# A banded-attention pass: v and the first scores moved ahead of the products with v, those put inside the k projection, half of the next x asked for later

## The reference, cut to what matters

```python
h = rms_norm(x, ln_g[l])
proj = jnp.einsum('bsd,de->bse', h, w_in[l])
(u_pool, g_pool, c_a, c_b, g_conv, q, k, v, g_attn) = split_columns(proj)
...
y_attn = sliding_window_attention(q, k, v, attn_sinks[l])   # 8 heads, 2 kv heads, window 128, ALiBi, sinks
y = jnp.concatenate([y_pool * jax.nn.silu(g_pool), y_conv * jax.nn.silu(g_conv), y_attn * jax.nn.silu(g_attn)], axis=-1)
x = x + jnp.einsum('bse,ed->bsd', y, w_out[l])
return rms_norm(x, final_g)
```

## Time and profile before

| | |
|---|---|
| median of 3 runs | 1409.57 us (1408.69 to 1409.6) |
| the profiled execution | 1410.81 us |
| its span, first to last instruction | 1409.1 us |
| mean granted TensorE clock | 0.991 of full speed |
| PE busy | 1362.0 us of the span |
| DVE busy | 1143.6 us of the span |

### The profile page before, as it was taken

The page is one execution under the profiler, slowest core; times in us unless marked ns, Lnnn a source line. Parts: engine busy times, 40 slices in busy tenths (PEclk is TensorE's granted clock), DMA queues, the critical chain, the costliest instruction groups (busy, mean ns, idle before and its releaser), DMA issues.

```text
span 1409.1 us, 20603 instructions
## 1 busy us (share of the span) xinstructions
PE 1362.0 (97%) x7070; PEld 1115.8 (79%) x7070; DVE 1143.6 (81%) x2173; ACT 550.5 (39%) x1421; POOL 480.5 (34%) x745
## 2 busy tenths in 40 slices
PE   6999999999999999989999999999999999999998
PEld 5778777777778787768888888888888888888886
DVE  5787868686868685629899998988999998898886
ACT  5665656564646463412112122121232333333332
POOL 5363636272726362530101011010110355455552
PEclk9999999999999999999999999999999999999999
DMA  9749494949494848774203133031327575554531
GB/s 214 217 124 316 125 325 112 314 129 309 126 295 146 252 153 199 284 158 180 115 35 135 37 129 134 15 134 59 144 97 261 232 249 169 180 179 158 169 106 75
DMA packets 117547, 239.18 MB, mean 170 GB/s; under 512 B 17488, under 2 KB 75216, under 8 KB 109776
## 3 DMA queue, kind: packets, MB, share of 16 engines
q1 hardware_dynamic: 93312, 214.24, 45.8%
q10 hardware_dynamic: 24144, 23.80, 7.0%
HBM read 139.44 MB, written 98.57 MB: 169 GB/s over the span
## 4 chain that ended last, share of the span: by engine, by line
PE 70%; DVE 13%; DMA 10%; SPq 3%; issue 2%; POOL 1%; ACT 0%; POOLq 0%; DVEq 0%; ACTq 0%
PE wide L346 12%; PE wide L348 12%; PE wide L347 12%; DMA p_scratch<-a_rows 7%; PE pair L1290 4%; PE pair L1291 4%; PE pair L1296 4%; DVE xT L339 4%; DVE m_tail L2076 3%; PE wide L1323 2%; PE turn L1257 2%; PE pair L348 2%; PE turn L347 2%; PE turn L348 2%; PE pair L347 2%
## 5 line engine op out<-in xcount | busy, mean ns | idle before, releaser
L2076 DVE SCALAR_TENSOR_TENSOR m_tail<-m_tail,m_taps 128x512 f32<-128x512 f32 x480 | 337.5, 748 | 4.6
L1818 POOL TENSOR_TENSOR operand_sums<-m_y 128x512 f32<-128x512 f32 x75 | 102.5, 1367 | 167.4 <-PE wide L348 116.2
L1296 PE MATMUL pair<-xT,w_hi 128*128 128x512 f32 x384 | 154.5, 402 | 3.9 <-DVE xT L339 2.3
L1290 PE MATMUL pair<-xT,w_hi 128*128 128x512 f32 x384 | 152.3, 397 | 3.6 <-DVE w_lo L410 3.6
L1291 PE MATMUL pair<-xT,w_lo 128*128 128x512 f32 x384 | 151.7, 395 | 0.0
L108 POOL TENSOR_TENSOR pool_carrier<-pool_carrier 128x1 f32<-128x1 f32 x23 | 14.0, 611 | 395.2 <-DVE m_meanvar L2085 395.2
L346 PE MATMUL wide<-x_first,w_hi 128*128 128x512 f32 x320 | 125.4, 392 | 0.0
L346 PE MATMUL wide<-xT,w_hi 128*128 128x512 f32 x320 | 125.2, 391 | 0.0
L348 PE MATMUL wide<-x_first,w_hi 128*128 128x512 f32 x320 | 124.6, 389 | 0.0
L347 PE MATMUL wide<-x_first,w_lo 128*128 128x512 f32 x320 | 124.5, 389 | 0.0
L348 PE MATMUL wide<-xT,w_hi 128*128 128x512 f32 x320 | 124.5, 389 | 0.0
(11 more groups left out here) (266 smaller groups left out, 3220.7 us busy)
## 6 DMA issues: line engine op xcount, KB each, us to landing
xT_scratch<-xT SPq DMA_DIRECT2D x16, 2048.0 KB, 10.2
p_scratch<-a_rows SPq DMA_DIRECT2D x128, 128.0 KB, 2.8
x_first<-xT_scratch SPq DMA_DIRECT2D x16, 1024.0 KB, 9.0
xT<-xT_scratch SPq DMA_DIRECT2D x16, 1024.0 KB, 9.7
combo_scratch<-stage SPq DMA_DIRECT2D x28, 512.0 KB, 5.7
m_y<-y_scratch ACTq DMA_DIRECT2D x14, 1024.0 KB, 6.6
xs<-in_x_dram SPq DMA_DIRECT2D x20, 512.0 KB, 10.3
a_pT<-p_scratch SPq DMA_DIRECT2D x16, 512.0 KB, 3.6
```

The lines of the kernel that those rows point to most:

```text
L1290: nc.tensor.matmul(out, w.hi(c)[:, kk, cols], st.hi[:, kk, :], start=(kk == 0), stop=False)
L1296: last = nc.tensor.matmul(out, w.hi(c)[:, kk, cols], st.lo[:, kk, :], start=False, stop=(kk == KT - 1))
L1818: nc.gpsimd.tensor_tensor(operand_sums[:, i, 1], y_block(q, left), y_block(q, right), SIGN[op]).then_inc(operand_sum, 1)
L2076: nc.vector.scalar_tensor_tensor(out=conv[:, i, :], in0=h[:, i, j:j + TB], scalar=taps[:, i, j:j + 1], in1=conv[:, i, :], op0=ALU.mult, op ...
```

## The change

On PE, v comes behind q3, with the fold of the next x's squares inside it, then the scores of tile 0 with all heads together, and then `attend(n-1, 1)`. The scores of tiles 1, 2 and 3 each stand inside a projection (g0, g1, g2), behind its fourth row tile (`CUT = 3`). `attend(n-1, 0)` goes into k of block n, between all its hi matmuls and all its lo matmuls. On SP, the half of the next x is asked for behind the store and the load of the probabilities' fourth tile. The squares go behind q_hi(2) on ACT and behind q_lo(2) on DVE, the mean behind q_lo(3), the combos of slots 3 and 4 behind that, and POOL's root ahead of the mask of tile 3. On ACT, v is taken ahead of all exponentials, and each tanh stands behind both halves of a tile's exponentials.

```diff
+CUT = 3
...
@@ -735,12 +735,12 @@
...
             else:
-                st.load(sp, n + 1, (0, 1))
                 load_probs(sp, n - 1, 2)
                 for s in combos.of_block(n, (0,)):
                     combos.store(sp, s)
                 store_probs(sp, n - 1, 3)
                 load_probs(sp, n - 1, 3)
+                st.load(sp, n + 1, (0, 1))
...
@@ -879,10 +879,11 @@
             if n == 0:
                 make_seen()
             else:
-                for j in (2, 3):
-                    mask(n - 1, j)
+                mask(n - 1, 2)
             if n < NB - 1:
                 st.root(pool, n + 1, carrier)
+            if n > 0:
+                mask(n - 1, 3)
...
@@ -972,9 +973,6 @@
             q_hi(n, 0)
             if first:
                 w.split_hi(act, CHUNK_Q + 1)
-            elif not final:
-                act.wait_ge(free(slot("g3")), earlier(n - 1, slot("g3")) + 1)
-                st.square(act, n + 1)
...
                 w.load(act, CHUNK_GP, (2, 3))
             make_combos((2,))
             q_hi(n, 2)
-            make_combos((3,))
+            if not first and not final:
+                act.wait_ge(free(slot("g3")), earlier(n - 1, slot("g3")) + 1)
+                st.square(act, n + 1)
             if first:
                 w.split_hi(act, CHUNK_G + 1)
             elif final:
                 w.split_hi(act, CHUNK_CB)
             q_hi(n, 3)
-            make_combos((4,))
...
                 for part in (0, 1):
                     st.scale(act, n + 1, part)
-                exps(n, 0, 0)
-                sink_exp(n, 0, 0)
-                take_v()
-                exps(n, 0, 1)
-                sink_exp(n, 0, 1)
+            take_v()
+            for kv in range(KV):
+                soft(0, kv)
+            if not final:
                 st.scale(act, n + 1, 2)
-                exps(n, 1, 0)
-                sink_exp(n, 1, 0)
+            for kv in range(KV):
+                soft(1, kv)
+            if not final:
                 act.wait_ge(st.squared_more, st.HALF * (n + 1))
-                gate_tanh(n, 0)
-                exps(n, 1, 1)
-                sink_exp(n, 1, 1)
+            gate_tanh(n, 0)
+            if not final:
                 st.scale(act, n + 1, 3)
-                spread_v()
-                exps(n, 2, 0)
-                sink_exp(n, 2, 0)
-                gate_tanh(n, 1)
-                exps(n, 2, 1)
-                sink_exp(n, 2, 1)
+            spread_v()
+            soft(2, 0)
+            soft(2, 1)
+            gate_tanh(n, 1)
+            if not final:
+                exps(n, 3, 0)
                 gate_tanh(n, 2)
                 for kk in (0, 1):
                     st.split_hi(act, n + 1, kk)
-                exps(n, 3, 0)
+                sink_exp(n, 3, 0)
+                soft(3, 1)
                 for kk in range(2, st.AHEAD):
                     st.split_hi(act, n + 1, kk)
                 gate_tanh(n, 3)
                 st.split_hi(act, n + 1, KT - 1)
-                sink_exp(n, 3, 0)
-                exps(n, 3, 1)
...
@@ -1154,71 +1140,65 @@
                 w.split_lo(dve, CHUNK_Q, 0)
...
+            if not first:
+                for name in ("g2", "g3"):
+                    dve.wait_ge(free(slot(name)), earlier(n - 1, slot(name)) + 1)
+                output(dve, n - 1, 0)
             make_k_lo(n)
-            if not first:
-                output(dve, n - 1, 0)
             make_combos(n, (0,))
             if not first:
                 turn_squares_of_probs(SUB * n - 1)
             make_q_lo(n, 0)
-            if not first and not final:
...
             for t in range(1, GROUP):
-                make_combos(n, (t,))
+                if t < 3:
...
-                if t == 3 and not final:
-                    for s in combos.of_block(n, (4,)):
-                        combos.add(dve, s)
...
-                if t == 2 and not final:
-                    st.mean(dve, n + 1)
+                if t == 2 and not first and not final:
+                    st.square_more(dve, n + 1)
...
+            if not final:
+                st.mean(dve, n + 1)
+            make_combos(n, (3, 4))
...
             for kv in range(KV):
                 take_scores(n, 0, kv)
+            for part in (0, 1):
+                next_x(part)
             if not first:
                 output(dve, n - 1, 1)
+            take_scores(n, 1, 0)
...
@@ -1298,15 +1278,18 @@
                     last.then_inc(st.spent, 1)
                 return last
 
-            lag = K_LAG if name == "k" and n > 0 else 0
-            for kk in range(KT):
-                by_hi(kk)
-                if kk >= lag:
-                    last = by_lo(kk - lag)
-                if between and kk < KT - 1:
-                    between(kk)
-            for kk in range(KT - lag, KT):
-                last = by_lo(kk)
+            if name == "k" and n > 0:
+                for kk in range(KT):
+                    by_hi(kk)
+                attend(pe, n - 1, 0)
+                for kk in range(KT):
+                    last = by_lo(kk)
+            else:
+                for kk in range(KT):
+                    by_hi(kk)
+                    last = by_lo(kk)
+                    if between and kk < KT - 1:
+                        between(kk)
...
             need(pe, score_taken, 2 * (m - 1) + 2)
-            late = (HEADS - 2, HEADS - 1) if j == 0 else ()
             for h in range(GROUP):
                 by_k_lo(h)
-                if h + GROUP not in late:
-                    by_k_lo(h + GROUP)
+                by_k_lo(h + GROUP)
...
-                    if h not in late:
-                        last = by_k_hi(h)
...
             def once(kk):
-                if kk == (4 if n == 0 else 1):
+                if kk == 1:
...
                 st.first_transposes(pe)
                 project(n, "k", lambda kk: st.transpose(pe, kk + TURNS) if kk + TURNS < KT else None)
-            else:
-                attend(pe, n - 1, 0)
             for name in ("q0", "q1", "q2", "q3"):
-                project(n, name, folding(n) if name == "q3" and not final else None)
+                project(n, name)
+            project(n, "v", None if final else folding(n))
+            pe.wait_ge(q_taken, GROUP * (n + 1))
+            scores(n, 0)
             if not first:
                 if not final:
                     pe.wait_ge(st.rstd_steps, st.chain(n + 1, 2))
                 attend(pe, n - 1, 1)
-            pe.wait_ge(q_taken, GROUP * n + 3)
-            scores(n, 0)
-            project(n, "v")
+            project(n, "g0", after(CUT, lambda: scores(n, 1)))
+            project(n, "g1", after(CUT, lambda: scores(n, 2, lambda: turn_v(n))))
+            project(n, "g2", after(CUT, lambda: scores(n, 3)))
+            project(n, "g3")
             if final:
-                scores(n, 1)
-                project(n, "g0")
-                scores(n, 2, lambda: turn_v(n))
-                project(n, "g1")
-                scores(n, 3)
-                project(n, "g2")
-                project(n, "g3")
                 attend(pe, n, 0)
             else:
-                project(n, "g0", after(2, lambda: scores(n, 1)))
-                project(n, "g1", after(4, lambda: scores(n, 2, lambda: turn_v(n))))
-                project(n, "g2")
-                scores(n, 3)
-                project(n, "g3")
                 project(n + 1, "k")
 
```

More of the change, by code:

```diff
@@ L52 @@
 PIECE = 4
-K_LAG = 3
+CUT = 3
 PIECES = KT // PIECE
@@ L1037, in body @@
                 st.split_hi(act, n + 1, KT - 1)
[L1038 to L1055 removed]
+            else:
                 w.split_hi(act, CHUNK_GP)
                 for kv in range(KV):
[L1058 to L1059 removed]
+                    soft(3, kv)
                 for t in (2, 3):
@@ L1178, in body @@
                     join_bias()
-                if t == 2 and not final:
-                    st.mean(dve, n + 1)
+                if t == 2 and not first and not final:
+                    st.square_more(dve, n + 1)
                 if final and t >= 2:
                     w.split_lo(dve, CHUNK_CB + t - 2)
-            for s in combos.of_block(n, (4,)):
-                combos.split_lo(dve, s)
+            if not final:
+                st.mean(dve, n + 1)
+            make_combos(n, (3, 4))
             def next_x(part):
-                st.turn_squares(dve, n + 1, part)
+                if not final:
+                    st.turn_squares(dve, n + 1, part)
             for kv in range(KV):
                 take_scores(n, 0, kv)
+            for part in (0, 1):
+                next_x(part)
             if not first:
                 output(dve, n - 1, 1)
-            if not final:
-                for part in (0, 1):
-                    next_x(part)
-                take_scores(n, 1, 0)
-                turn_squares_of_probs(SUB * n)
-                take_scores(n, 1, 1)
-                next_x(2)
-                gate_make(n, 0)
-                take_scores(n, 2, 0)
```

(42 more changed lines are left out.)

24 lines of the change are left out of this document (5 added, 19 removed).

## The result

The changed kernel takes 1438.61 us (median of four runs, 1436.53 to 1441.69), the kernel before 1409.59 beside it: a ratio of 1.0208, with a 95% interval of 1.0186 to 1.0231. It is 2.1% slower, and 1.6 us from the 1437.0 predicted. Its profiled execution has a span of 1435.3 us at a mean granted clock of 0.984, against 1409.1 and 0.991.

A forecast was written before the change was run, and what follows sets the result against it. PE, busy 97% of the span, was taken as the bound. A block of 34.5 + 43 = 77.5 against 72.86 gave +28 over six, block 0 0, last block -1: +27 on 1410.81, median 1437 us, range 1405 to 1460.

The forecast's parts named there:

- x's place: Loads of the next x: landing at +23.6 us behind the block's first q0 matmul, against +12.65 before; bounds +22.5 and +27.
- The fold's wait: Inside v, PE stalls 3.5 us at the fold, wanted at +23.5, for x's squares, done at +26.9.
- The clock: Behind the 3.5 us stall in v, PE's lower granted clock costs 1.4 to 2.5 us more; 1.8 taken.
- T: DVE's first take_scores of a block, counted from its first q0 matmul: +32.7, or +34.5 us with the low clock.
- From T to the next zero: From DVE's first take_scores to the next block's first q0 matmul: 43 us, bounds 39.4 and 44.5, against 44.06 before.
- The sum: A block 77.5 us against 72.86, +28 over six blocks; with block 0 and the last block, +27 in total.
- Block 0: The first block: up to 5 us of PE's waits go, DVE's first take_scores comes 3 later; taken as 0 (-4 to +3).
- the last block: Mask 3 no longer stalls it and the closing chain of stores and loads begins 1 us earlier: -1 (-4 to +3).
- The first: Rival: tile 2's store shares engines with ACT's x, or SP's chain is shorter; x at +19.5, some 1391 us; chance 0.10.
- step (b): Tile 2's store stands behind ACT's half of x on the same DMA engines, landing 9.98 behind ACT's issue, at +6.5.
- The second: Rival: x late, but 40.5 us behind DVE's first take_scores and the clock hardly falls; some 1408 us; chance 0.18.
- The fourth: Rival: store 3 at its upper bound, x at +27, clock low in v and scores; 1465 us and more; chance 0.06.

The follow-up runs named there:

- experiment 1: The changed kernel with SP's half of the next x asked for at its old place, ahead of tile 2's load: 1399.06 us, ratio to before 0.9923.
- experiment 5: The changed kernel with the fold 12 matmuls later in v and x as late: 1432.95 us, ratio to before 1.0166.
- 8: The kernel of experiment 1 with the first two tanhs put back between the halves of tile 1's and tile 2's exponentials: 1392.3 us, ratio to before 0.9876.
- experiment 4: The changed kernel with all four parts of the next x asked for by ACT, none by SP: 1398.58 us, ratio to before 0.9923.

## Why the prediction was right, step by step

**x's place.** Predicted for block 2 and measured: ACT asks at -3.5, -4.8; tile 2's store landed at +6.5, +5.2; tile 3's landed at +13.7, +12.5; SP asks at +15.2, +14.0; x landed at +23.6, +23.0; the fold at +26.9, +26.6. All of it began 1.3 early, and every interval held but x's last: 9.0 from issue to landing, not 8.4. That SP's store lands 9.98 behind ACT's issue was measured as 10.02. The chosen value for a store without the rest of x ahead of it (7.2 behind the store before it, in bounds of 6.2 and 10.8) came out as 7.3.

**The fold's wait.** 3.5 predicted; 3.35 in block 2 and 3.92 on the mean, with 5.5 in block 5, the longest of the kernel before too.

**The clock.** 1.8 predicted; experiment 1 gives 2.25 a block on the mean, and block 2 lost 2.9.

**T.** +34.5 predicted, +35.3 measured in block 2, where the low clock took 2.9 (7.27 against 4.41 for the same matmuls in experiment 1). The half us for the mask, which the prediction has behind T's scores, did not come, since PE was slower than the mask. The chain beside it was as long as it was said to be (mask of tile 3 done at +33.4, predicted +33.6), and experiment 5 shows that it is what bounds PE next.

**From T to the next zero.** 43 predicted, 42.37 measured. PE's loss at k's head to ACT's hi splits is there, some 1.8 for 1.5 (16 matmuls from 243.68 to 249.07, 5.39 for 3.63); that to the lo splits is gone. Two terms have the measured waits behind them: DVE waited 1.2 and 1.15 for the tanhs, and moving these gave 1.1 a block back (experiments 1 and 8).

**The sum.** A block 77.5, measured 77.54. So close a hit is in part luck: in block 2 T is 0.8 too late and the stretch behind it 0.6 too short, and the six blocks run from 76.45 to 79.04. Block 0 was taken at 0 and came out at +0.9, the last block at -1 and -2.35. These two errors offset each other as well, and both steps were mis-sized. In block 0 PE's wait for q's lo part went, as said, but 5.6 us for DVE's maxima came in three places; in the last block the wait for the maxima shrank from 3.5 to 2.6 and the last masks' grew from 5.6 to 7.7.

**The rivals.** The first had x by +19.5, by the turns that "DMA: Bandwidth & Descriptors" in the Trainium skill describes. Queues do move side by side (experiment 4), but in the changed kernel SP's moved nothing until some 0.9 of ACT's 1.05 MB was through, so step (b) of the prediction held. Its threshold of +20.2 fits: x at +19.4 cost 0.95 a block, x at +23.0 cost 6.24. Its block for an early x, 69.1 to 72.1, is what experiment 1 measured, 71.3; its 1391 us took 4 us in block 0 that did not come (zero of block 1 at 99.91 there, 98.73 before) and a mean block of 70.6. The second (a short stretch behind T, the clock hardly lower) fell on both counts: 42.37 and not 40.5, and 2.9 of low clock in block 2. The fourth needed x at +27.

## What to carry to other kernels

A load is not off the path because nothing reads it for 20 us: count from its landing through everything that the first reader's result is queued ahead of, and look for the step at which the slack ends: here the price was 0.95 a block on one side of it and 6.24 on the other. When a wait is moved from one engine to the next and the sum of PE's waits stays (30.7, 31.1, 29.5), look upstream for the common source first: mending it won 39.5 us here, the two moves of the wait 5.7 and 7.5. A change of several parts can hide a gain behind a loss: here one line of it cost 39.5 us and the rest won 10.5, and a transposition placed "too early" on a busy engine may be what frees a buffer two tiles on.

## What the runs showed of the hardware that was not expected

A store of four pieces, issued some 1 us behind the loads on the other queue, moves nothing for 4.4 us and more, and then lands in part ahead of the last of these loads (experiment 4). And a short wait can lower PE's clock. In experiment 5, behind 1.83 us at the fold, windows of block 2 show

```profile
204.88:206.95 2.07, 2.07 (x9) 1.24 (x9) 1.61 (x4) 0.95 (x2) 0.01 (x1) 0.83 0.91 312
206.95:208.50 1.55, 1.55 (x11) 1.33 (x11) 0.85 (x2) 0.88 (x2) 1.55 (x1) 0.50 1.19 497
```

a granted clock of 0.83 and then 0.50 over v's end and the first scores, where 1.68 in front of the products with v left 1.00 in the kernel before. The second wait of that block, 1.72 at the mask, comes only behind these windows. Length alone does not decide: blocks 4 and 6 wait longer, 0.9 and 3.1, 0.4 and 2.6, and PE is busy for 70.44 and 70.40 in them at a clock of 1.00. What sets these apart isn't settled here. On the mean of the six blocks the clock costs 1.4 (71.43 of busy PE, 70.05 in experiment 1), where the single wait of the changed kernel costs 2.25.
